# Products of ones on the tensor engine in the prologue of a hybrid decoder layer

## The reference

```python
def rmsnorm(x, g):
    xf = x.astype(jnp.float32)
    y = xf * lax.rsqrt(jnp.mean(xf * xf, axis=-1, keepdims=True) + EPS)
    return (y * g.astype(jnp.float32)).astype(x.dtype)
...
    n1 = rmsnorm(x, norm_mix)
    proj = n1 @ w_in
    z, xbc, dt_raw, sc_b, sc_c, sc_h, gate_a, gate_b = split_last(proj, IN_SPLITS)
```

## Time and profile before

| | us |
|---|---|
| median of 3 runs | 3033.98 |
| lowest, highest | 3030.57, 3037.28 |
| the profiled execution, its own time | 3030.75 |
| its span, first to last instruction | 3029.0 |

### The profile page before, as it was taken

The page is one execution under the profiler, slowest core; times in us unless marked ns, Lnnn a source line. Parts: engine busy times, 40 slices in busy tenths (PEclk is TensorE's granted clock), DMA queues, the critical chain, the costliest instruction groups (busy, mean ns, idle before and its releaser), DMA issues.

```text
span 3029.0 us, 53137 instructions
## 1 busy us (share of the span) xinstructions
PE 2927.2 (97%) x20000; PEld 2875.4 (95%) x20000; DVE 1724.6 (57%) x2181; ACT 1144.1 (38%) x1642; POOL 382.7 (13%) x617
## 2 busy tenths in 40 slices
PE   7899999999999999999999999899999999999988
PEld 6899999899999999999999999899999999999988
DVE  7565657566565755554555454755555555555564
ACT  4343434344343433333333333433333333333443
POOL 2332313133231310000000000100000000000101
PEclk9899999999999999999999999999999999999999
DMA  6465555556555565555555555355455555555543
GB/s 194 124 175 141 163 166 151 164 144 173 143 171 164 147 188 148 147 151 152 148 144 153 153 147 153 112 153 150 145 148 152 148 143 152 152 146 150 158 129 107
DMA packets 753334, 458.20 MB, mean 151 GB/s; under 512 B 14634, under 2 KB 747234, under 8 KB 752626
## 3 DMA queue, kind: packets, MB, share of 16 engines
q1 hardware_dynamic: 669184, 396.61, 46.3%
q10 hardware_dynamic: 83345, 56.99, 6.5%
q0 software_dynamic: 672, 2.66, 0.2%
HBM read 430.73 MB, written 25.47 MB: 151 GB/s over the span
## 4 chain that ended last, share of the span: by engine, by line
PE 87%; DVE 6%; issue 3%; ACTq 1%; ACT 1%; POOL 1%; DMA 0%; DVEq 0%; POOLq 0%; SPq 0%
PE ps L1464 27%; PE ps L1466 27%; PE ps L1465 27%; PE ps L1780 2%; DVE wlo L926 1%; PE ps L1765 1%; PE ps L1754 1%; PE ps L1742 1%; DVE cv L1026 1%; POOL wm L1386 1%; DVE nt L944 1%; DVE var L1167 1%; PE ps L1775 0%; ACT whi L608 0%; PE ps L1616 0%
## 5 line engine op out<-in xcount | busy, mean ns | idle before, releaser
L1464 PE MATMUL ps<-n_hi,whi 128*128 128x320 f32 x4240 | 1330.2, 314 | 51.3 <-DVE wlo L926 20.3
L1465 PE MATMUL ps<-n_lo,whi 128*128 128x320 f32 x4240 | 1321.3, 312 | 0.0
L1466 PE MATMUL ps<-n_hi,wlo 128*128 128x320 f32 x4240 | 1320.9, 312 | 0.0
L926 DVE TENSOR_TENSOR wlo<-raw,whi 128x1024 fp32r<-128x1024 f32 x747 | 928.1, 1251 | 566.7 <-ACT whi L608 566.3
L608 ACT ACTIVATE whi<-raw 128x1024 fp32r<-128x1024 f32 x747 | 784.0, 1056 | 904.0 <-PE ps L1466 858.3
L1464 PEld LDWEIGHTS ps<-n_hi,whi 128*128 128x128 f32 x4240 | 806.7, 190 | 57.8 <-issue 32.8
L1465 PEld LDWEIGHTS ps<-n_lo,whi 128*128 128x128 f32 x4240 | 806.7, 190 | 0.6
L1466 PEld LDWEIGHTS ps<-n_hi,wlo 128*128 128x128 f32 x4240 | 805.9, 190 | 0.0
L1464 PE MATMUL ps<-c_hi,whi 128*128 128x320 f32 x1728 | 535.5, 310 | 3.3 <-DVE c_lo L1019 3.1
L1465 PE MATMUL ps<-c_lo,whi 128*128 128x320 f32 x1728 | 534.6, 309 | 0.0
L1466 PE MATMUL ps<-c_hi,wlo 128*128 128x320 f32 x1728 | 534.6, 309 | 0.0
(11 more groups left out here) (272 smaller groups left out, 1743.6 us busy)
## 6 DMA issues: line engine op xcount, KB each, us to landing
raw<-in_w_in SPq DMA_DIRECT2D x322, 512.0 KB, 5.2
raw<-in_w_ffn_gate SPq DMA_DIRECT2D x88, 512.0 KB, 4.7
raw<-in_w_ffn_up SPq DMA_DIRECT2D x88, 512.0 KB, 4.9
raw<-in_w_ffn_down SPq DMA_DIRECT2D x88, 512.0 KB, 4.0
raw<-in_w_ssm_out SPq DMA_DIRECT2D x64, 512.0 KB, 4.3
h<-in_state_ssm ACTq DMA_DIRECT2D x32, 512.0 KB, 4.5
out_ssm_sample<-hn ACTq DMA_DIRECT2D x32, 512.0 KB, 4.9
raw<-in_w_sc_out SPq DMA_DIRECT2D x32, 512.0 KB, 4.1
```

The costliest lines, as they stand in the source:

```text
L926: tt(wlo[slot][:], raw[slot][:], whi[slot][:].bitcast(F32), SUB).then_inc(lo_split, 1)
L1464: mm(out, w_h, x_h, start=first, stop=False)
L1465: mm(out, w_h, x_l, start=False, stop=False)
L1466: return mm(out, w_l, x_h, start=False, stop=last)
```

## The change

ACT copies ones into the first 640 columns of `whi[3]`, the slot that is used last, right behind its 14 transfers, and signals `warm_ready`. PE waits for that and makes products of them, each 128 x 128 by 128 x 512, into bank 7, which nobody reads until the dt unit writes it: 10 before everything else, 6 ahead of each of the groups 1, 2 and 3 of the transposes, 4 before it waits for `rstd_ready`, and 14 behind the spreading of the factor. The last signals `warm_done`, for which ACT waits before it writes weights into `whi[3]`. The transposed gain moves from bank 7 to bank 6.

```diff
@@ ACT, split_hi
+                    if seg.name == "prologue" and slot == 3:
+                        act.wait_ge(warm_done, 1)
                     wait(act, multiplied, n - RING + 1)
                     activate(whi[slot][:], raw[slot][:], copy).then_inc(hi_split, 1)
@@ ACT, start
                 act.wait_ge(consts_ready, 1)
+                activate(whi[3][:, 0:5 * P].rearrange("p (a b) -> p a b", b=P),
+                         ones[:].unsqueeze(1).broadcast_to([P, 5, P]), copy).then_inc(warm_ready, 1)
                 activate(rcol[:, 0:1], ones[:, 0:1], ACT.Sqrt)
@@ DVE, start
                 dve.wait_ge(g1_turned, 1)
-                v.tensor_copy(g1col[:], ps[:, 7, 0:KM]).then_inc(g1_kept, 1)
+                v.tensor_copy(g1col[:], ps[:, RMS_BANK[1], 0:KM]).then_inc(g1_kept, 1)
@@ PE
+            def keep_warm(n):
+
+                for _ in range(n):
+                    last = mm(ps[:, DT_BANK, :], whi[3][:, 0:P], whi[3][:, P:5 * P], start=True, stop=True)
+                return last
...
                 if kind == "start":
+                    pe.wait_ge(warm_ready, 1)
+                    keep_warm(10)
                     pe.wait_ge(ident_ready, 2)
                     pe.wait_ge(g1_loaded, 16)
-                    turn(ps[:, 7, 0:KM], grow[:], ident[0:KM, 0:KM]).then_inc(g1_turned, 1)
+                    turn(ps[:, RMS_BANK[1], 0:KM], grow[:], ident[0:KM, 0:KM]).then_inc(g1_turned, 1)
                     for k in range(KM):
+                        if k % 4 == 0 and k:
+                            keep_warm(6)
                         if k % 4 == 0:
                             pe.wait_ge(x_loaded[k // 4], 32)
...
                         last.then_inc(x_turned, 1)
+                    keep_warm(4)
                     pe.wait_ge(rstd_ready, 1)
...
                     last.then_inc(rstd_spread, 1)
+                    keep_warm(14).then_inc(warm_done, 1)
```

More of the change, by code:

```diff
@@ L330, in hybrid_decoder @@
         ident_ready, consts_ready, zeroed = sem("ident_ready"), sem("consts_ready"), sem("zeroed")
+        warm_ready, warm_done = sem("warm_ready"), sem("warm_done")
         x_turned, x_kept_a, x_kept_v = sem("x_turned"), sem("x_kept_a"), sem("x_kept_v")
```

## The result

The changed kernel takes 3045.98 us (median of 5 runs, 3043.32 to 3050.11) against 3033.48 (median of 5, 3030.57 to 3037.28): ratio 1.0043, 95% interval 1.0028 to 1.0057, so 12.5 us or 0.4% slower. The forecast was slower by 5.9 us, 3039.9, with a range of 3035 to 3047. The sign was right and the time lies in the range; the size was half of what came. The profiled execution took 3043.32 us with a span of 3041.6, 12.6 more than the profiled one before.

What follows compares the result with a forecast made beforehand. In the first 21 us the arrival of x, PE's transposes and DVE's queue share the bound. +9.7 us late start, 3.9 given back, small corrections: +5.9 on 3033.98 makes 3039.9 us, range 3035 to 3047.

Steps and rivals of the forecast that it cites:

- rival 3: Transposes of x: clock rises and falls between the groups, part of the transposes cost 0.306 again; +8 to +12, chance 0.05.
- DVE's groups took over 3.5 us: Sign of a wrong forecast, in DVE's squares of x; groups were expected 2.7 to 2.9 us apart.
- When the ones are ready: Prologue: ACT's copy ends at 11.25 us behind 14 transfers and a table load; PE starts at about 11.4.
- The ten products: PE's start: 4.3 us, mostly or all at the low clock; DVE starts squares at 16.2 instead of 6.49, +9.7 us.
- Rival 2: Prologue: the ten products don't raise the clock, everything runs at 1.2 GHz; +16.4 us, 3050, chance 0.09.
- Does PE keep up?: Groups of x: 12 transposes and six products take PE 2.8 us, just DVE's 2.74; +5.9 us at group 3's squares.
- the 9.7 us of late start: DVE's first squares, 16.2 instead of 6.49 us; 3.9 us were to come back by group 3.
- the +5.8 of that step: DVE's groups from 16.2 us, at 2.74 us each, end at 24.4 against 18.59.
- The high clock in the dt unit: Dt unit's products: faster clock worth nothing because DVE sets that time; bounds 0 and -1.8 us.
- From there on all moves along: Everything behind group 3's squares shifts by the same +5.9 us; remaining products and the new wait are covered.
- Rival 4: Later PE waits fall otherwise against the clock: not slower or faster, +1.6 or -1.1 us; chance 0.08, 0.03 for gain over 0.2%.

Runs made afterwards that it cites:

- the early ones: The changed kernel with DVE instead of ACT making the ones, all 46 products kept: 3037.47 us against 3030.78 for the kernel before, ratio 1.0022.
- the small products: The kernel before plus 23 tiny two-pass products (46 instructions) behind the spreading of the factor, nothing else: 3040.54 us against 3031.49, ratio 1.0030.

## Why the prediction was right in sign and short by half

That the time fell into the range of 3035 to 3047 is in part luck. Its upper end was there for rival 3, which did not happen; the time came near it by the two failed steps below. And one sign of being wrong that the prediction names did appear: DVE's groups took over 3.5 us (3.72).

**When the ones are ready: right.** Table load, copy of 0.74 us (0.7 estimated), second load hidden, PE's first product at 10.8 (11.4 forecast; ACT got through its transfers 0.6 us sooner). The price of this wait alone was measured at +4.4 us at the dt unit. The copy starts 0.02 us behind the load. The drain that the Trainium skill adds to each switch ("ScalarE: Activation LUTs", What ACT_TABLE_LOAD costs) does not show here either.

**The ten products: right.** 4.0 us against 4.3, and they did lift the clock. Rival 2 did not happen.

**"Does PE keep up?" is the first step that failed.** It took the 0.116 us of the transposes at line 1635 for those of x at the high clock. They take 0.19. With the products (1.50 us for six, forecast 1.4) a group is then 3.72 us and not 2.8, PE and not DVE sets the pace, and of the 9.7 us of late start less came back. Group 3 comes 10.65 us behind the first squares, forecast 8.2; less the 1.1 us by which DVE started sooner, this turns the +5.8 of that step into +7.15. Taking out the products between the groups restored 2.73 us a group. The two are not "of the same kind", as the prediction has it: all nine of line 1635 are full blocks, and of x every third has 64 rows. The step between full blocks is 0.108 us in both; the steps into and out of a shorter one are 0.20. Three steps make 0.51 us and four tiles 2.05 of the 2.23. Why such a step costs double, no run shows.

**Rival 3, the fall between groups, did not happen.** Transposes alone did not raise the clock (14.7 us), but they held it for 9.7 us in the run without the middle products. The Trainium skill ("TensorE: Matmul & The Clock Gate", Part 4, PE-mode transpose) says that the full clock does not engage in them; for the rise the traces agree, for the holding they don't.

**The high clock in the dt unit: right, worth nothing.** It was lost in the 4 us wait anyway, and DVE's `n_lo` set the time.

**"From there on all moves along" is the second step that failed**, by 5.4 us. This was argued from data flow alone. Prices of instructions were counted, their number not: 46 product instructions ahead of the loops make ACT's issues in the ssm loop long (48 us of waits over six rounds against 45) and cost about 6.8 us with nothing else changed. With 64 the issues are short and the loss in the loops is 19 us, of which 13 are the two turns of the short-convolution loop. Pure delays of 4.4 and 8.6 us cost 3.3 and 9.3 in the medians, so it is not the delay. Rival 4 looked for luck of the clock; the long issues came back in all four profiles with 46 (the changed kernel twice, the early ones, the small products), and in none of the others.

What the number moves, queue 8 shows: loads of instructions, 16 KB at a time. In the kernels with nothing but small products only PE's program grew, so the place of the loads against the loops follows PE's count. With 46 they fall on ACT's issues; with 64 the short-convolution loop, which ran its later rounds without a load, needs one about every 19 us, and at its turns PE stands still while two follow each other by some 3 us. The same pairs stand at the turns of the ssm loop in the kernel before: PE's 2.15 us of "issue" ahead of 301.10 lie between loads at 298.0 and 301.6. This is a coincidence in time, but it is seen at every stop and long issue named here, and in these kernels nothing but the count moved it. What stays open is how a load makes ACT's issue longer, and why one beside it at times does not. Of the 5.4 us, ACT's queue accounts for 3.3 over six rounds; the rest lies in the ssm rounds too, but was not put down to single waits.

## What to carry to other kernels

Before work is put into a wait, look at what it must wait for itself: here the ones stood behind 14 transfer issues, and a gap of PE was filled by making the work behind it late. Put filler only where an engine idles and stop there; the 18 products between the groups served a clock that was not in danger and made PE the pace. And when a change adds instructions ahead of a loop, measure the same number of idle instructions alone, since their count can cost as much as the work. The page's row of instruction loads is a first sign: here its packets rose from 106 to 125 when a loop had begun to load in every round. With 46 they did not rise, and only their place had moved.

## What the runs showed that I had not expected

- Transposes of x at the high clock: 0.19 to 0.20 us against 0.306 at the low one. They hold the clock once it is up (9.7 us) but didn't raise it (14.7 us).
- At the high clock a transpose follows another of 128 rows after 0.108 us; into and out of one of 64 rows it takes 0.20.
- A product of 16 columns in two passes took 0.22 us per instruction at the low clock (46 in 9.99 us), hardly less than 320 columns of the rounded type (0.267).
- Product instructions ahead of the loops, with nothing else changed: 28 cost 2.8 us, 46 cost 9.05 (2.3 of it their own time), 64 cost 25.4 (6.1 their own); 46 behind the loops 3.2. The 2.8 and the 3.2 go with a lower mean clock.
- The profile shows loads of instructions, 16 KB each, on queue 8. Twelve of ACT's transfer issues in the changed kernel that began up to 0.6 us behind the start of such a load took 0.9 to 1.7 us instead of 0.5 to 0.65.
